# Moving a forget gate from its own stage into the projection stage of a two-layer decoder step

## What is computed

```python
def fox_project(h, w_in, b_f):
    q, k, v, fg = jnp.split(h @ w_in, B_SPLITS, axis=-1)
    logf = jax.nn.log_sigmoid(fg.astype(jnp.float32) + b_f.astype(jnp.float32))
...
def fox_prompt(h, w_in, b_f, w_o):
    q, k, v, logf = fox_project(h, w_in, b_f)
    c = jnp.cumsum(logf, axis=1)
```

## Time and profile before

| | |
|---|---|
| median of the runs shown | 1859.73 us |
| the profiled execution, own time | 1840.43 us |
| its span | 1838.6 us |
| PE busy | 1615.8 us (88%) |
| DVE, ACT, POOL busy | 802.1, 675.6, 144.1 us |
| mean granted clock of PE | 0.916 |
| moved by DMA | 189.53 MB, mean 103 GB/s |

### The profile page before, as it was taken

The page is one execution under the profiler, slowest core; times in us unless marked ns, Lnnn a source line. Parts: engine busy times, 40 slices in busy tenths (PEclk is TensorE's granted clock), DMA queues, the critical chain, the costliest instruction groups (busy, mean ns, idle before and its releaser), DMA issues.

```text
span 1838.6 us, 31069 instructions
## 1 busy us (share of the span) xinstructions
PE 1615.8 (88%) x12244; PEld 1439.5 (78%) x12244; DVE 802.1 (44%) x1731; ACT 675.6 (37%) x1211; POOL 144.1 (8%) x273
## 2 busy tenths in 40 slices
PE   4698958889888999999999768999888999998996
PEld 3485447778487999998899747778487999998995
DVE  0234957777335334333353413444335333334443
ACT  2433324335214433334333433445315333334334
POOL 0312011111101000000000311111101000000000
PEclk9699668889898999999999878889898999999998
DMA  6515920002442544554131013002441222222211
GB/s 184 173 42 164 315 98 24 23 0 115 183 138 70 172 158 136 175 182 148 51 127 48 29 34 113 23 0 115 183 161 47 92 91 91 91 80 74 90 38 47
DMA packets 154361, 189.53 MB, mean 103 GB/s; under 512 B 6789, under 2 KB 148269, under 8 KB 149974
## 3 DMA queue, kind: packets, MB, share of 16 engines
q1 hardware_dynamic: 143906, 144.65, 24.6%
q0 software_dynamic: 5600, 36.24, 5.3%
q10 hardware_dynamic: 4768, 7.42, 1.3%
HBM read 183.65 MB, written 4.83 MB: 103 GB/s over the span
## 4 chain that ended last, share of the span: by engine, by line
PE 72%; DVE 11%; issue 8%; ACT 5%; DMA 2%; ACTq 0%; DVEq 0%; POOL 0%; SPq 0%; POOLq 0%
PE ps L515 52%; PE ps L1067 3%; PE ps L1136 2%; PE ps L1118 2%; DVE arena L983 2%; PE ps L539 2%; DVE small L982 1%; PE ps L1086 1%; PE ps L598 1%; DVE arena L1297 1%; PE ps L1127 1%; PE ps L1406 1%; PE ps L1352 1%; DMA const<-in_const 1%; DVE rt L620 1%
## 5 line engine op out<-in xcount | busy, mean ns | idle before, releaser
L515 PE MATMUL ps<-hH,wH 128*128 128x260 f32 x2592 | 534.9, 288 | 59.0 <-DVE hL L666 38.5
L515 PE MATMUL ps<-hH,wL 128*128 128x260 f32 x2592 | 529.1, 286 | 0.0
L515 PE MATMUL ps<-hL,wH 128*128 128x260 f32 x2592 | 528.8, 286 | 0.0
L515 PEld LDWEIGHTS ps<-hH,wH 128*128 128x128 f32 x2592 | 407.7, 192 | 67.0 <-issue 64.7
L499 DVE TENSOR_TENSOR wL<-ring,wH 128x1024 fp32r<-128x1024 f32 (+1 forms) x172 | 203.7, 1188 | 560.8 <-ACT wH L493 560.7
L515 PEld LDWEIGHTS ps<-hH,wL 128*128 128x128 f32 x2592 | 406.9, 192 | 0.0
L515 PEld LDWEIGHTS ps<-hL,wH 128*128 128x128 f32 x2592 | 406.8, 192 | 0.0
L493 ACT ACTIVATE wH<-ring 128x1024 fp32r<-128x1024 f32 (+1 forms) x184 | 188.8, 1029 | 593.1 <-PE ps L515 576.5
L1202 ACT ACTIVATE arena<-arena 128x128 f32<-128x128 f32 (+3 forms) x128 | 72.2, 564 | 185.4 <-DVE arena L1283 101.4
L1118 PE MATMUL ps<-arena 68*128 (+4 forms) x256 | 101.6, 488 | 7.5 <-DVE arena L1183 2.6
L1136 PE MATMUL ps<-arena 128*128 (+1 forms) x640 | 91.3, 276 | 14.0 <-ACT arena L1210 13.5
(11 more groups left out here) (258 smaller groups left out, 1795.0 us busy)
## 6 DMA issues: line engine op xcount, KB each, us to landing
ring<-in_w_ada SPq DMA_DIRECT2D x48, 1024.0 KB, 9.7
ring<-in_w_up SPq DMA_DIRECT2D x44, 1024.0 KB, 5.1
ring<-in_w_down SPq DMA_DIRECT2D x16, 1024.0 KB, 5.5
ring<-in_w_in_a SPq DMA_DIRECT2D x8, 1024.0 KB, 7.5
ring<-in_w_down SPq DMA_DIRECT2D x8, 768.0 KB, 4.5
ring<-in_w_in_b SPq DMA_DIRECT2D x6, 1024.0 KB, 5.4
ring<-in_w_o_a SPq DMA_DIRECT2D x4, 1024.0 KB, 9.0
ring<-in_w_o_b SPq DMA_DIRECT2D x4, 1024.0 KB, 9.0
```

The lines of the kernel that those rows point to most:

```text
L515: ins = pe.matmul(ps[:, 2 * p + half, 0:HT], w[:, h, kc, t * P:t * P + P], mov[:, k0 + kc, half * HT:half * HT + HT], start=(first and kc ...
```

## The change

- The third panel of the head stage goes. Its place takes a load of 32 columns (the last 16 of the values and the 16 gate columns), used without a split: after the key panel PE multiplies it with the unsplit activations in four column groups (`pe_fdots`, 16 matmuls). Between the halves of the value panel five matmuls add the four partial sums and turn them to token-major (`pe_fsum`).
- The gate's chain (`act_gate`, `dve_gate`) is done in the head stage, after the second key tile in ACT's order. PE's transposes of the past and the cumulative sums follow the turns of the tiles (`pe_past`, `pe_cum`, `pe_cumq`). The sums by key are formed once for 16 heads, into 16 partitions; the sums by query are turned from them. ACT spreads them over the four key/value heads with a scale that is zero for other heads, so `hsel` has 16 rows (128 KB instead of 32 KB, in both layers) and the contraction has 80 rows instead of 68.
- POOL does its modulation first, then the memsets and `hsel`, then the gathers of the gate values, waits for them, and copies keys after that.
- The key store is issued in the middle of the stage, the `logf` stores behind it, the value store at its end. The first query panel is split in the head stage.
- The gate stage and its barrier go. What is left of it (copies of the sums and of the past, scan and bias) stands at the head of the attention stage (`act_cum`, `dve_cum`).
- The constants grow by 27 columns.

```diff
-            ("head1", [(s, W) for s in (3, 0, 1)], 1),
+            ("head1", [(s, W) for s in (3, 0)], 1),
+            ("fg1", [(1, W)], 1),
...
+        def pe_fdots(pe):
+
+            s = panel_ready(pe, "fg1", 0, 0)
+            for k0 in (0, 4):
+                for half in range(2):
+                    for q in range(4):
+                        ins = pe.matmul(ps[32 * q:32 * q + 32, 6 + half, 0:HT], panel_view(s)[:, k0 + q, 0:32],
+                                        hT[:, k0 + q, half * HT:half * HT + HT], start=(k0 == 0), stop=(k0 == 4))
+            ins.then_inc(S("fg_dot"), 1)
+            pe.sem_inc(S(f"ring_free{s}"), 1)
+
+        def pe_fsum(pe):
+
+            pe.wait_ge(S("fg_raw"), 1)
+            pick = const[:, K_SUM + NH:K_SUM + 2 * NH]
+            for q in range(QT):
+                pe.matmul(ps[:, 5, q * NH:q * NH + NH], fgraw[:, q * P:q * P + P], pick, start=True, stop=True)
+            pe.matmul(ps[0:NS, 5, QT * NH:QT * NH + NH], fgraw[:, SEQ:TOK], pick, start=True, stop=True).then_inc(S("fg_sum"), 1)
...
+        def pe_cum(pe):
+
+            pe.wait_ge(S("hd1_raw"), 3)
+            pe.wait_ge(S("lf_done"), 1)
+            for kb in range(QT):
+                ins = pe.matmul(ps[HD:HD + NH, 0, kb * P:SEQ], lf[:, kb, :], const[:, K_TRI + 384:K_TRI + 384 + SEQ - kb * P],
+                                start=(kb == 0), stop=(kb == QT - 1))
+            ins.then_inc(S("lf_ck"), 1)
+            pe.wait_ge(S("lf_x"), 1)
+            pe.transpose(ps[:, 1, P:P + NS], lgx[0:NS, :], ident[0:NS, 0:NS]).then_inc(S("lf_xt"), 1)
+
+        def pe_cumq(pe):
+
+            pe.wait_ge(S("lf_cks"), 1)
+            for q in range(QT):
+                ins = pe.transpose(ps[:, 1, q * NH:q * NH + NH], ckS[HD:HD + NH, q * P:q * P + P], ident[HD:HD + NH, HD:HD + NH])
...
+        def act_gate(act):
+
+            z, e = zf.rearrange("p (t h) -> p t h", t=5), zg.rearrange("p (t h) -> p t h", t=5)
+            act.wait_ge(S("fg_dot"), 1)
+            act.activation(v520(fgraw), pair(3), ACT.Copy).then_inc(S("fg_raw"), 1)
+            act.wait_ge(S("lf_z"), 1)
+            act.activation(e, z, ACT.Abs).then_inc(S("lf_act"), 1)
...
+        def act_cum(act):
+
+            act.wait_ge(S("lf_ck"), 1)
+            for g in range(NKV):
+                act.activation(kaug[HD:HD + NH, g, 0:SEQ], ps[HD:HD + NH, 0, :], ACT.Copy, scale=const[HD:HD + NH, K_HG + g:K_HG + g + 1])
...
+                        if l == 1 and (t, h) == (2, 0):
+                            pe_fsum(pe)
+                    if l == 1 and t == 0:
+                        pe_fdots(pe)
...
+                    if l == 1:
+                        if u == 0:
+                            pe_past(pe)
+                        elif u == 1:
+                            pe_cum(pe)
+                        elif u == 3:
+                            pe_cumq(pe)
...
+                if l == 1:
+                    if t == 1:
+                        act_gate(act)
+                    if t == 3:
+                        keep(ktok, knew, "k", 2, "k_out")
+                        act.wait_ge(S("lf_done"), 1)
+                        act.dma_start(O["logf_p"].rearrange("(t p) c -> p t c", p=P), lf[:, 0:QT, :]).then_inc(S("stores"), 16)
+                        act.dma_start(O["logf_s"], lf[0:NS, QT, :]).then_inc(S("stores"), 16)
+                    if t >= 4:
+                        split_high(act, "q1", 0, 0, t - 4)
+            if l == 1:
+                keep(Vt, vnew, "v", 4, "stores")
+                act.wait_ge(S("k_out"), 32)
...
-            K = HD + GR
+            K = HD + NH
...
-                in_turn(pool, pool.memset(Qz[:, :, :, :], 0.0))
+                if l == 0:
+                    pool_fixed(pool, l)
+                pool_mod(pool, 2 * l, ada[:, base:base + KC, :])
                 if l == 1:
-                    in_turn(pool, pool.memset(lf[:, :, :], 0.0))
-                else:
-                    in_turn(pool, pool.memset(kaug[64:68, :, 0:SEQ], 0.0))
-                pool.dma_start(qst[HD:HD + GR, :, 0:SEQ], I["hsel"]).then_inc(S("in_hsel"), 16)
-                pool.wait_ge(S("in_hsel"), 16 * (l + 1))
-                pool_mod(pool, 2 * l, ada[:, base:base + KC, :])
+                    pool_fixed(pool, l)
+                if l == 1:
+                    slot_free(pool, "logf", 0, 0)
+                    for b in range(NS):
+                        gather_logf(pool, b)
+                    pool.wait_ge(S("past_full2"), fill("logf", 0, 0)[2])
                 pool_head(pool, l)
```

More of the change, by code:

```diff
@@ L317, in build, with early @@
         ssm = part(16)
-        lfT = part(PAST + 1, work0)
-        cs = part(PAST + 1)
-        lgx = part(P)
-        zf = part(5 * NH)
-        zg = part(5 * NH)
+        otflat = OT.rearrange("p k t -> p (k t)")
+        at[0] = A_N - KC * TOK
+        def early(n, lo=[0]):
+            lo[0] += n
+            assert lo[0] <= KC * TOK
+            return otflat[:, lo[0] - n:lo[0]]
+        lfT = early(PAST + 1)
+        cs = early(PAST + 1)
+        lgx = early(P)
+        zf = early(5 * NH)
+        zg = early(5 * NH)
+        fgraw = early(TOK)
+        ckS = early(SEQ)
         gT = part(FC * TOK, 0).rearrange("p (k t) -> p k t", k=FC)
@@ new lines, in pe_fsum, with pe_past @@
+        def pe_fsum(pe):
[4 more added lines that the diff above has]
+            pe.matmul(ps[0:NS, 5, QT * NH:QT * NH + NH], fgraw[:, SEQ:TOK], pick, start=True, stop=True).then_inc(S("fg_sum"), 1)
+        def pe_past(pe):
+            slot, before, _ = fill("logf", 0, 0)
+            pe.wait_ge(S(f"ring_free{slot}"), before + 1)
+            pe.wait_ge(S("lf_z"), 1)
+            for n in range(NPG):
+                ins = pe.transpose(ps[:, 4 + n // 4, (n % 4) * P:(n % 4) * P + P], cs[:, n * P:n * P + P], ident)
+            ins.then_inc(S("lf_turn"), 1)
@@ new lines, in pe_cumq @@
+        def pe_cumq(pe):
+            pe.wait_ge(S("lf_cks"), 1)
+            for q in range(QT):
+                ins = pe.transpose(ps[:, 1, q * NH:q * NH + NH], ckS[HD:HD + NH, q * P:q * P + P], ident[HD:HD + NH, HD:HD + NH])
+            ins.then_inc(S("lf_cq"), 1)
+        def act_gate(act):
[4 more added lines that the diff above has]
+            act.activation(e, z, ACT.Abs).then_inc(S("lf_act"), 1)
+            act.wait_ge(S("lf_act"), 1)
+            act.activation(e, e, ACT.Exp, scale=-1.0).then_inc(S("lf_act"), 1)
+            act.wait_ge(S("lf_act"), 2)
+            act.activation(e, e, ACT.Ln, bias=ones[:, 0:1]).then_inc(S("lf_act"), 1)
@@ L806, in dve_head, with pool_fixed @@
                 dve.tensor_tensor(out, sq[0:rows, 0, :], sq[0:rows, 1, :], ALU.add).then_inc(S(f"{tag}_fm"), 1)
+            if l == 1:
+                dve_gate(dve)
+                for h in range(2):
+                    split_low(dve, "q1", 0, 0, h)
+        def pool_fixed(pool, l):
+            in_turn(pool, pool.memset(Qz[:, :, :, :], 0.0))
+            if l == 1:
+                in_turn(pool, pool.memset(zf, 0.0))
+            else:
+                in_turn(pool, pool.memset(kaug[HD:HD + NH, :, 0:SEQ], 0.0))
+            pool.dma_start(qst[HD:HD + NH, :, 0:SEQ], I["hsel"]).then_inc(S("in_hsel"), 16)
+            pool.wait_ge(S("in_hsel"), 16 * (l + 1))
         def pool_head(pool, l):
@@ L1219, in units @@
                     to_place(n + 1)
-            for h in range(2):
-                split_high(act, f"q{l}", 0, 0, h)
+            if l == 0:
+                for h in range(2):
+                    split_high(act, "q0", 0, 0, h)
+            else:
+                act_cum(act)
             for t in range(2):
@@ L1305, in units @@
                 turned_outputs(g, n, QT - 1)
-            for h in range(2):
-                split_low(dve, f"q{l}", 0, 0, h)
-            for t in range(2):
-                if l == 0:
+            if l == 0:
+                for h in range(2):
+                    split_low(dve, "q0", 0, 0, h)
+                for t in range(2):
                     rope(n0, t)
+            else:
+                dve_cum(dve)
             to_place(n0)
@@ L1421, in act_samp @@
         def act_samp(act, l):
+            if l == 1:
+                act.wait_ge(S("stores"), 16 * STORES[2])
             for m in range(0, 16, 2):
```

160 lines of the change are left out of this document (64 added, 96 removed).

## The result

| | before | after |
|---|---|---|
| median of the runs, us | 1859.16 (4 runs, 1853.73 to 1860.52) | 1815.62 (4 runs, 1814.46 to 1817.19) |
| ratio, 95% interval | | 0.9772 (0.9750 to 0.9793) |
| profiled execution, own time and span, us | 1840.43 and 1838.6 | 1814.97 and 1813.1 |
| reciprocal to query panel in the profile, us | 80.3 | 49.3 |

The kernel became 43.5 us faster; 31.7 was forecast (1828). The two profiled executions differ by only 25.5.

A forecast was written before the change was run, and what follows sets the result against it. TensorE was taken to bound the kernel. Savings of 32.0 us less 0.35 for larger tables gave -31.7, put on the 1859.7 median: 1828 us, range 1817 to 1838.

The forecast's parts named there:

- Step 1: Start of layer 1: with GpSimd's modulation first, the splits start earlier; -2.2 us.
- Steps 2 and 3: Head stage: gate dots in four column groups, 2.0 us, and sums over groups between value panel halves, 1.2 us.
- Rival (d): The gate dots' column groups run one by one: +6 to 10 us, 1836; chance 0.03.
- Step 4: The gate's chain beside the value panel costs nothing, with nearly 2 us of slack for ScalarE.
- Step 5: The third panel, 48 matmuls and 5.78 us, goes, with its evacuation, turns and split.
- Step 6: Tail from value panel to query panel, which starts at 1070.8 instead of 1102.76; -32.0 us in all up to here.
- rival (a): TensorE's clock falls in the tail before the query panel: 1831; chance 0.17.
- (b): The tail before the query panel is longer, by 3 to 9 us: say 1834; chance 0.11.
- (c): TensorE's clock stays up until the query panel, whose 3.60 us at 0.50 shrink by half: 1826; chance 0.05.
- (e): The gate stage goes, but its wait returns whole as a DMA wait behind the barrier: 1860; chance 0.02.
- (f): Slower: gathers hold ScalarE in the gate and the value panel's evacuation waits: 1870; chance 0.02.
- Step 7: Copies, scan and bias moved behind the barrier are covered by the first query tile and cost nothing.

The follow-up runs named there:

- e2: The changed kernel, unchanged, run and profiled again: 1814.33 us, ratio 0.9757.
- e6: The changed kernel with one of the eight gathers of cached gate values (seven sequences left out): 1812.36 us, ratio 0.9750.
- e4: The changed kernel with layer 1's memsets and hsel fetch put back ahead of GpSimd's modulation: 1819.15 us, ratio 0.9779.
- e3: The kernel before with only GpSimd's layer 1 modulation moved ahead of its memsets and hsel fetch: 1851.45 us, ratio 0.9952.
- e9: The changed kernel with the gate's dots and the sums over column groups each issued twice: 1821.63 us, ratio 0.9808.
- e14: The changed kernel with layer 0's index-key gathers issued early, run beside the unchanged changed kernel: 1814.74 us, ratio 0.9781.
- e1: The kernel before, unchanged, run and profiled once more: 1859.92 us, ratio 1.0002.
- e10: The changed kernel with the cumulative sums over the keys issued four times: 1823.68 us, ratio 0.9816.
- e11: The changed kernel with ScalarE's six copies and VectorE's scan and bias moved back ahead of the barrier: 1825.49 us, ratio 0.9821.
- e15: The kernel before, unchanged, one run for another profile: 1856.92 us.
- e16: The kernel before, unchanged, one further run for a profile: 1856.29 us.
- e5: The kernel before with one of the eight gathers of cached gate values (seven sequences left out): 1847.70 us, ratio 0.9949.
- e13: The changed kernel, unchanged, run again on another chip: 1818.75 us, ratio 0.9808.
- e7: The kernel before with the eight gate gathers issued ahead of GpSimd's key copies: 1858.88 us, ratio 1.0000.
- e12: The changed kernel with layer 0's eight index-key gathers issued before GpSimd's index-key copies: 1814.69 us, ratio 0.9773.

## Why the prediction was right or wrong

**Step 1, right.** -2.2 forecast, -2.4 measured at the first low half.

**Steps 2 and 3, nearly right.** The dots took 1.90 us (1.96 forecast) and the sums over groups 0.94 without stalls in e2 (1.2). Doubling both cost 3.2. Rival (d), column groups one by one, falls. The 60 cycles a matmul of the Trainium skill (TensorEngine Tiling (Array Packing), Instruction Overhead) would alone give 0.3 for the sums over groups, an estimate; the trace has three times that.

**Step 4, wrong in its slack and in what it left out.** I forecast nearly 2 us of slack for ScalarE. With one gather (e6) it was 2.0. In e2 ScalarE ended the gate at 1062.68 and the value panel was through at 1062.77: the slack was 0.1, since the last gather's values landed near 1058.2 and the bias add came 1.5 us later than forecast. Where TensorE stalls, the panel ends later and ScalarE waits for it, 2.95 us in the first profile. So the slack was never used up. GpSimd's wait for `hsel` was 4.1 to 4.7 us in the profiles that issue it right ahead of the gathers, where I had 2.93. Its fourfold size is not the reason. In e4, where it is issued ahead of the modulation, the same 128 KB landed as fast as 32 KB did before:

```profile
1033.16 2.91 DMA arena<-in_hsel
```

In e3 the old 32 KB, issued where the changed kernel issues it, took 4.6 us, beside the load of the next weight panel. The place made the wait longer. What the step left out is that TensorE stalls and slows beside the gathers: 49.3 us in the stretch against 46.5 in e2, and 46.0 with one gather. In the first profile the stalls hold 1.4 us, and the panel's second half takes 7.47 us at a mean granted clock of 0.77. In e6, with one gather, it takes 5.95 us at 1.00:

```profile
1056.31 5.95 PE ps L529 x48
```

The first profile and e9 to e14 show the stalls as the changed kernel's usual state, about 3 us.

**Step 5, right as far as it goes, mis-sized.** The third panel was 5.78 us in the profile that I read, but 7.29 in e1, with 3.7 us more of waiting ahead of it.

**Step 6, right.** From the value panel's end to the query panel I forecast 11.5 us; the profile has 10.0 (1067.00 to 1076.99). The cumulative sums took 2.26 us (2.6), and in e10 three more cost 6.5 in the chain. The clock stayed at 1.00 in this tail, so rival (a) falls as it was meant, and (b) too. At the start of the query panel it was low (0.57), so (c) falls; no wait for DMA came back behind the barrier (e), and no gather landed late enough to make the kernel slower (f).

**Step 7, right.** With the cover taken away (e11), what it hid cost 7.3 us.

**Step 8.** Too small to see: the landing of the constants varies by itself from 15.2 to 17.4 us across the profiles of both kernels.

**What failed is the last line, the sum's transfer.** It reads: "I put the same -31.7 on them". All durations came from one execution, 19 us under the median, and I treated that gap as something that both kernels share. 6 us of it are not shared. They were a hold in the very stretch that the change rebuilds, present in all three other profiles of that kernel (86.2 in e1, 86.3 in e15, 86.4 in e16) and absent in the one that I read. The changed kernel moves its gathers so that no evacuation of a panel falls late in them. So typical profiles give 86.3 - 49.2 = 37.1 us. That is, to a tenth, the forecast's own 32.0, plus the 6.0 that were missing, plus 2.3 from terms each a little too pessimistic (34.3 by e5 and e6), less the 3.3 (49.2 - 46.0) that TensorE's stalls give back. That the first two profiles differ in the stretch by 31.0, close to the forecast's 32.0, is in part luck: the one of before lacked the hold, and the one of after had the stalls, which the forecast did not know.

The measured difference is 43.5 at first, 45.6 by the medians of e1 and e2, and 35.6 by e13 on another chip (0.9808 against 0.9757: these intervals don't meet). About 6 us of the 43.5 stay open, and the record narrows them in two ways. First, by their spans the three profiles of either unchanged kernel (1854.5, 1855.0, 1854.5 and 1813.1, 1811.5, 1814.2) are 40.3 to 43.5 us apart, and 3 to 5 of these lie outside the stretch. The query panels behind it hold some 0.8 of them (142.0 in e15 against 141.2 in the first profile of after). Of the 3.2 between e1 and e2, the landing of the constants is 1.6 (17.39 against 15.76), which is chance. Second, the runs of before fall in two groups, near 1855 and near 1860. On the chip of e1 and e2, 13 of 15 lie in the upper one, on that of e13, 6 of 9 in the lower, and this makes over half of the distance from 45.6 to 35.6; the rest is the changed kernel's own (1814.33 and 1818.75). What makes the upper group was not found: the three later profiles of before all stand at 1856 or 1857, so that none shows it.

## What to carry to other kernels

Hold the profiled execution's own time against the median of the runs before you sum from it. If it lies under them, something is missing in it. Don't take this for a common offset unless a second profile shows that it lies outside the stretch that the change rebuilds; without one, widen the range to that side by the gap. When you place a row of indirect gathers, look at which engine's releases fall in their last microseconds, not only at who needs the data. A chain piece whose releaser the profile cannot name is worth a search for what ends with it.

## What the runs showed of the hardware

Beside eight GpSimd gathers (10 us of issue, 1.25 us each), TensorE's releases reached ScalarE late. Releases up to 1.9 us after the start of the first gather were prompt (e1, e2, e7). Those at 2.7 to 3.3 us after it (the copy of the dots) were late by 1.5 to 2.1 us. Later ones, while gathers were still being issued, were late by 2.4 to 6 us, and one that came just after the last issue by 0.9 (e12), but none reached ScalarE more than 1.7 us after the end of the last gather's issue. In layer 0 VectorE got a release of TensorE 1.6 us late as well (e1, e2), while a release of ScalarE reached VectorE at once (e4). In the same time TensorE itself could go on with its turns (e1) or stall for 0.4 to 0.9 us at a time (e9, e10, e11). With one gather left in layer 1 neither was seen there. Of all profiles with eight gathers only the first one of the kernel before shows no held release, in layer 0 and in layer 1. Why was not found, nor whether TensorE's stalls are late fetches of instructions: no run takes the one without the other.

Four column groups of 32 columns ran beside each other at 0.06 us a record (32 in 1.90 us, against 0.28 us a record without groups), with the group changed at each matmul. Small matmuls with a load of 128 weight columns took 0.09 to 0.11 us a record.
